# The weight parts' loads on SyncE's queue, ScalarE's copy of the turned keys, a later norm turn and a later pooled-input copy in one decoder layer

## The reference

```python
hn = rmsnorm(h, g_attn_norm[i])
z = hn @ w_in[i]                  # 512 q, 128 k, 128 v, 512 pooled input u
q = rmsnorm(q.reshape(B, S, N_Q_HEADS, HEAD_DIM), g_q[i])
...                               # k likewise; window 128, sinks, shared bias
# multiscale_pool_mixer: trailing mean over 2/4/8/16 positions minus the token,
# then a 128x128 map for each of the 4 groups, and a scale for each channel
y = jnp.einsum('bsgc,gcd->bsgd', pooled, w_pool.astype(jnp.float32))
...
```

## Time and profile before

| | |
|---|---|
| runs | 2050.17, 2062.04, 2053.68 us; median 2053.68 |
| profiled execution | 2053.4 us, span 2051.5 us |
| granted clock of PE | 0.998 of full speed |
| busy | PE 2011.2 us (98%), DVE 67%, ACT 44%, POOL 20% |
| end of the row stages on PE | about 558 us |
| w_lo on DVE (L1554) | 68 of them, 1.287 us in the mean |
| w_parts<-w_split | 88 DMAs of 512 KB on POOL's queue, 4.8 us from issue to landing |

### The profile page before, as it was taken

How to read it: one execution, slowest core, us unless ns; L and a number is a source line. 1 busy time by engine, 2 the same in 40 slices (tenths; PEclk the granted TensorE clock), 3 DMA queues, 4 the chain that set the end, 5 groups by cost and what they waited for, 6 DMA issues and landing times.

```text
span 2051.5 us, 26122 instructions
## 1 busy us (share of the span) xinstructions
PE 2011.2 (98%) x9546; PEld 1663.4 (81%) x9546; DVE 1372.9 (67%) x1920; ACT 899.7 (44%) x1460; POOL 406.5 (20%) x508
## 2 busy tenths in 40 slices
PE   8999999999999999999999999999999999999998
PEld 6887878877788888888888878788888888888877
DVE  4696674767696665655888765966566566987663
ACT  4575754657433333333333543533333333334542
POOL 4454644645410000000000220000000000001310
PEclk9999999999999999999999999999999999999999
DMA  7757566364934223225825128432322328352143
GB/s 193 201 180 245 188 236 219 130 236 131 347 127 130 81 72 103 72 72 171 307 62 165 36 72 223 143 119 67 96 85 72 100 79 292 130 159 78 42 134 103
DMA packets 197387, 292.09 MB, mean 142 GB/s; under 512 B 16139, under 2 KB 118452, under 8 KB 195980
## 3 DMA queue, kind: packets, MB, share of 16 engines
q1 hardware_dynamic: 172672, 212.97, 34.1%
q0 software_dynamic: 22176, 76.96, 10.8%
q10 hardware_dynamic: 2412, 0.50, 0.1%
HBM read 223.25 MB, written 67.51 MB: 142 GB/s over the span
## 4 chain that ended last, share of the span: by engine, by line
PE 84%; DVE 6%; DMA 3%; issue 3%; ACT 2%; POOL 1%; SPq 0%; ACTq 0%; DVEq 0%; POOLq 0%
PE bank L2623 13%; PE bank L2627 13%; PE bank L2625 13%; PE bank L2660 7%; PE bank L2661 7%; PE bank L2662 7%; PE bank L2323 4%; PE bank L2325 4%; PE bank L2324 4%; PE bank L2299 2%; PE bank L2301 2%; PE bank L2300 2%; DMA w_parts<-w_split 1%; PE bank L2392 1%; DVE w_lo L1554 1%
## 5 line engine op out<-in xcount | busy, mean ns | idle before, releaser
L2623 PE MATMUL bank<-a_hi,ring_hi 128*128 128x512 f32 x1232 | 479.7, 389 | 1.0 <-DVE ring_lo L1917 0.7
L2627 PE MATMUL bank<-a_hi,ring_lo 128*128 128x512 f32 x1232 | 479.3, 389 | 0.0
L2625 PE MATMUL bank<-a_lo,ring_hi 128*128 128x512 f32 x1232 | 479.3, 389 | 0.0
L2623 PEld LDWEIGHTS bank<-a_hi,ring_hi 128*128 128x128 f32 x1232 | 231.3, 188 | 49.9 <-DVE ring_lo L1917 1.4
L2625 PEld LDWEIGHTS bank<-a_lo,ring_hi 128*128 128x128 f32 x1232 | 231.3, 188 | 48.0
L2627 PEld LDWEIGHTS bank<-a_hi,ring_lo 128*128 128x128 f32 x1232 | 231.3, 188 | 47.8
L2660 PE MATMUL bank<-d_hi 128*128 128x512 f32 x616 | 239.8, 389 | 0.0
L2662 PE MATMUL bank<-d_hi,d_lo 128*128 128x512 f32 x616 | 239.7, 389 | 0.0
L2661 PE MATMUL bank<-d_lo,d_hi 128*128 128x512 f32 x616 | 239.6, 389 | 0.0
L1376 ACT ACTIVATE d_hi<-keep 128x1024 fp32r<-128x1024 f32 x132 | 139.8, 1061 | 201.9 <-PE bank L2662 184.9
L975 POOL DMA_DIRECT2D hidden_T<-hid x88 | 47.6, 541 | 770.4 <-DVE hid L1953 750.7
(11 more groups left out here) (258 smaller groups left out, 3879.9 us busy)
## 6 DMA issues: line engine op xcount, KB each, us to landing
w_parts<-w_split POOLq DMA_DIRECT2D x88, 512.0 KB, 4.8
hidden_T<-hid POOLq DMA_DIRECT2D x88, 256.0 KB, 2.3
raws<-in_w_gate SPq DMA_DIRECT2D x80, 256.0 KB, 4.7
raws<-in_w_up SPq DMA_DIRECT2D x80, 256.0 KB, 5.1
keep<-hidden_T SPq DMA_DIRECT2D x66, 256.0 KB, 3.8
raw<-in_w_ple_gate SPq DMA_DIRECT2D x64, 256.0 KB, 4.2
keep<-in_w_down SPq DMA_DIRECT2D x44, 256.0 KB, 4.4
other<-hidden_T SPq DMA_DIRECT2D x44, 256.0 KB, 6.8
```

Source lines behind the costliest of these rows:

```text
L2623: mm(dst[:, :], wh[:, g, cols], a_hi[o][:, k, :], start=fresh and k == 0, stop=False, skip_group_check=True)
L2625: mm(dst[:, :], wh[:, g, cols], a_lo[o][:, k, :], start=False, stop=False, skip_group_check=True)
L2627: ins = mm(dst[:, :], wl[:, g, cols], a_hi[o][:, k, :], start=False, stop=k == 3, skip_group_check=True)
```

## The change

Five edits, in the order of the diff:

1. `A_ORDER`, the order in which ACT makes the parts of the feed-forward input, is another.
2. `load_parts` is issued by SP in place of POOL, with the same waits, ahead of what else SP issues for the panel (behind `load_z` and `load_out`). Around it other loads stand elsewhere: the chunks of tile 3 in z(2) and no longer in out(1), the four `load_h(1)` in two panels, the four `load_a(0)` in four panels in place of two.
3. ACT copies the turned keys into SBUF as well (`k_raw`), ahead of `kT_hi`; DVE's `kT_lo` reads this copy; and PE's `transpose_probs`, which writes into the same bank 5, waits for `kT_hi` in place of `kT_lo`.
4. In the tiles 1 to 3 `copy_u` stands behind the half's hosted step, where that step does not begin a new pair of heads. Half 19 is as before.
5. In the gate section the turns of the norm of tile g+1, and what follows from them, stand one panel later.

No edit is to the pooled map itself (`pool_y`, `pool_y_hi`, `pool_y_rest`).

```diff
-A_ORDER = (0, 1, 3, 4, 2, 5, 6)
+A_ORDER = (0, 3, 4, 1, 2, 5, 6)
...
+        k_raw = sb_small("k_raw", [P, P])
...
+            def load_parts(i):
+                kept = (10 + i - OUT_AT[1] if OUT_AT[1] <= i < Z_AT[3] else i - Z_AT[2] if i < Z_AT[3] else
+                        i - Z_AT[3] if i < OUT_AT[2] else 10 + (i - OUT_AT[2]) % 8)
+                if i == SPLIT_END:
+                    sp.wait_ge(lo_done, SPLIT_END)
...
+                else:
+                    sp.wait_ge(panel_used, i - SLOTS_W + 1)
+                sp.wait_ge(parts_stored[kept % 2], 32 * (kept // 2 + 1))
+                for part in range(2):
+                    sp.dma_start(w_parts[parts_slot(i)][:, part, :].bitcast(F32), w_split[kept, part]
+                                   ).then_inc(parts_landed[parts_slot(i)], 16)
...
                 for c in range(10):
                     load_z(t + 1, c)
+                    if t == 1 and c == 0:
+                        load_parts(Z_AT[2] + 1)
+                    if t:
+                        load_parts(Z_AT[t + 1] + c + 2)
...
+                    if t == 1 and c == 9:
+                        for k in range(4):
+                            load_chunk(3, k)
...
                 for c in range(8):
                     load_out(t, c)
-                    if t == 1 and c == 0:
-                        for k in range(4):
-                            load_chunk(3, k)
-                        for b in range(NB):
-                            load_h(1, b)
+                    if t == 0 and c == 7:
+                        load_parts(Z_AT[2])
+                    if t:
+                        load_parts(OUT_AT[t] + c + 2)
+                    if t == 1 and c < 2:
+                        load_h(1, 2 * c)
+                        load_h(1, 2 * c + 1)
...
             for c in range(8):
                 load_out(3, c)
+                if OUT_AT[3] + c + 2 < ROW_PANELS:
+                    load_parts(OUT_AT[3] + c + 2)
                 if c == 0:
                     store_h1(2)
-                if c == 1:
-                    load_a(0, 0)
-                    load_a(0, 1)
-                    load_a(0, 3)
-                if c == 2:
-                    load_a(0, 2)
+                if 1 <= c < 5:
+                    load_a(0, (0, 2, 1, 3)[c - 1])
                 if c == 4:
                     store_n2(2, 0)
                     store_n2(2, 1)
...
-            def load_parts(i):
...
-                    pool.wait_ge(panel_used, i - SLOTS_W + 1)
-                pool.wait_ge(parts_stored[kept % 2], 32 * (kept // 2 + 1))
-                for part in range(2):
-                    pool.dma_start(w_parts[parts_slot(i)][:, part, :], w_split[kept, part]
-                                   ).then_inc(parts_landed[parts_slot(i)], 16)
...
+                if n:
+                    act.wait_ge(kstaged, n)
+                nc.scalar.activation(k_raw[:, :], bank[5][:, 0:P], ACT.Copy)
                 nc.scalar.activation(kT_hi[:, (b + 1) * P:(b + 2) * P], bank[5][:, 0:P],
                                      ACT.Copy).then_inc(k_hi_done, 1)
...
-                nc.vector.tensor_tensor(kT_lo[:, cols], bank[5][:, 0:P], kT_hi[:, cols].bitcast(F32),
+                nc.vector.tensor_tensor(kT_lo[:, cols], k_raw[:, :], kT_hi[:, cols].bitcast(F32),
                                         ALU.subtract).then_inc(kstaged, 1)
...
-                pe.wait_ge(kstaged, 4 * s + min((k + 1) // PAIRS + 1, NB))
+                pe.wait_ge(k_hi_done, 4 * s + min((k + 1) // PAIRS + 1, NB))
...
-                    for g in U_COPY_AT[t > 0].get(half, ()):
+                    fresh = any(has_unit(k, 0) and k % 2 == 0 for _, k in hosted_steps("z", t, half))
+                    u_first = fresh or half == 19 or not late
+                    for g in U_COPY_AT[t > 0].get(half, ()) if u_first else ():
                         copy_u(t, g)
...
                     hosted("z", t, half, Z_AT[t] + half // 2 + 1 if half % 2 == 0 and late else None)
+                    for g in () if u_first else U_COPY_AT[t > 0].get(half, ()):
+                        copy_u(t, g)
...
-                            if r == 1:
+                            if r == 2:
                                 sum_squares(NORM3[g + 1], bank[BS0[0]])
-                            if r == 2:
+                            if r == 3:
                                 normalise3(g + 1, 0)
                                 normalise3(g + 1, 1)
                                 norm3_lo(g + 1, 0)
-                            if r == 3:
                                 norm3_lo(g + 1, 1)
...
-                                if r == 0:
+                                if r == 1:
                                     pe.wait_ge(pp_copied, 8 * g + 4 + 1)
                                     turn_squares(NORM3[g + 1], acc3, bank[BS0[0]])
-                                if r == 1:
+                                if r == 2:
                                     pe.wait_ge(pp_copied, 8 * g + 4 + 2)
                                     turn_rstd(NORM3[g + 1], bank[BS0[1]])
```

More of the change, by code:

```diff
@@ L538, in store_n2 @@
                 sp.dma_start(hnT_d[t, :, 2 * b:2 * b + 2, :], normed(t, b)).then_inc(n2_stored[b % 2], 16)
+            def load_parts(i):
[3 more added lines that the diff above has]
+                    sp.wait_ge(lo_done, SPLIT_END)
+                elif i < SPLIT_END + SLOTS_W:
+                    sp.wait_ge(panel_used, SPLIT_END)
+                    for parity in range(2):
+                        sp.wait_ge(parts_stored[parity], 16 * (SPLIT_END - KEPT_FROM))
+                else:
[4 more added lines that the diff above has]
+                                   ).then_inc(parts_landed[parts_slot(i)], 16)
             def load_bias():
@@ L922, in z_section @@
                 for half in range(20):
-                    if t == 2 and half == 0:
-                        load_parts(Z_AT[2] + 1)
-                    if t >= 2 and half % 2 == 0:
-                        load_parts(Z_AT[t] + half // 2 + 2)
                     if t == 0 and half < 8:
@@ L952, in out_section @@
                 for half in range(16):
-                    if t == 0 and half == 14:
-                        load_parts(Z_AT[2])
-                    if t and half % 2 == 0 and OUT_AT[t] + half // 2 + 2 < ROW_PANELS:
-                        load_parts(OUT_AT[t] + half // 2 + 2)
                     if t < 2:
```

## The result

The changed kernel took 2067.69 us in the median of 7 runs (2066.65 to 2071.84), the kernel before 2052.86 in as many. The ratio is 1.0070, 95% interval 1.0057 to 1.0083: 14.4 us slower (the medians differ by 14.8). I had forecast 2049.5 with a range to 2059, so the sign and the range were wrong. The profiled execution took 2069.46 us, 16.1 more than that of before.

A forecast was written before the change was run, and what follows sets the result against it. PE bounds the kernel, busy 2011.2 of 2051.5 us, leaving 40.3 idle. Terms 3.6 + 4.2 - 2 - 0.5 - 1.4 = 3.9 us less than 2053.4 gave 2049.5 us, range 2043 to 2059.

The forecast's parts named there:

- What SP issues later: Norm stores behind parts on SP: 2 us more at the feed-forward start, 0.5 more in z(2) and z(3).
- The feed-forward start: First weights wait for stores behind panel 68's parts, leaving about 9 us ahead instead of 13.8: 2 us more, 0 to 9.
- A_ORDER: Feed-forward input: reordered ACT copies that no listed wait depends on; nothing gained or lost.
- The parts: Row stages: parts issued by SP end PE's waits for w_parts, 3.9 us, plus 0.3 behind them: 4.2 us less, 0 to 5.2.
- The rival with one queue and no gain: Parts queue behind SP's earlier transfers, so their stalls stay or move; parts' term nought, 2053.7 us, chance 0.14.
- Keys' copy and u copy: Attention in z(1) and z(3): stalls near 131, 153, 370 and 470 shrink; 3.6 us less, between 1.8 and 6.
- my 1.2 at 370 and 0.6 at 470: Keys' copy: logits start once qT_lo is ready, no longer after the kT_lo wait; 1.2 and 0.6 us less.
- The two waits for u at the pooled map: Behind the moved u copy, bank freed 2 to 4 us later, pooled sums later: nothing, up to 1 us lost.
- The norm turn: Two gate stages: PE still waits for w_lo, with transposes left to do; 1.4 us more, from 1 less to 4 more.
- The slower rival: Feed-forward start late because raws wait for norm stores that wait for panel 68: 2056.5 us, chance 0.16.
- its point of decision: Feed-forward start: the late start decides once first raws go less than about 6 us ahead of PE's start.

The follow-up runs named there:

- The first: The changed kernel with tile 3's chunk 4 to 7 loads in out(1) one panel earlier, ahead of the panel's weight parts: 2056.13 us, ratio 1.0013.
- third run: The kernel before with only the weight parts issued by SP and the loads placed as in the change: 2069.28 us, ratio 1.0072.
- ninth run: The changed kernel with chunk loads and out(3) norm stores ahead of parts, and the last two a_raw loads one panel earlier: 2053.41 us, ratio 0.9997.
- twelfth run: The kernel before with parts on SP, chunk loads, norm stores and a_raw loads earlier, and the new a_hi order; no other edit: 2053.84 us, ratio 0.9997.
- eighth run: The kernel before with only the gate section's norm turn one panel later: 2055.85 us, ratio 1.0016.
- fourth run: The kernel before with only the u copy moved behind the hosted step: 2051.80 us, ratio 0.9991.

## Why the prediction was wrong

**What SP issues later: the step that failed.** The term that I put at nothing is that of the chunk loads. I wrote that "SP now waits for PE at each panel from z(2) on, and what stands behind a pair of parts waits too", and then counted norm stores only. The chunk loads of out(1) stand behind such pairs, four of them, and there the load has no lead at all. I gave it nothing; it cost 9.6 us in the stretch from 320 to 346, and 12.9 when the 3.3 us of its first wait, ahead of 320, are counted in. The first and the third run settle it.

**The feed-forward start.** The mechanism was right, stores behind a pair of parts and the weights behind the stores, and I put it at 2 us with an upper bound of 9. It was 6.4. The pair for panel 70 left at 550.25, 16.3 us ahead of the start without PE's own wait, as I had worked out (16.4). But the pair and the two stores behind it took SP until 553.29 to issue, for which I had nothing, and the weights left 8.3 us behind them where I had 7.4. Part of the difference is another item of the same kind: I had costed the spread a_raw loads as a help for the parts and not as a delay for ACT. In the runs the stores are worth 3.0 us (6.9 to 3.9), 1.7 of it clock, and the a_raw loads 1.4 (3.9 to 2.5). In the ninth run's trace PE's waits from 536 to 600 are 1.45 us for the last parts and 0.82 for cg, so nearly all of the last 2.5; no run takes them away.

**A_ORDER.** "Moves copies on ACT that no row above waits for: nothing." It is worth 2.0 us in one pair of traces, by longer waits (4.2 us in place of 2.9) and a lower clock behind them, though the times of the two runs do not tell them apart. The reason is that the order of the loads changed with it: one edit could only be priced together with the other.

**The parts.** The waits in the earlier trace rows went, as forecast, 4.0 us. But 1.0 to 2.0 us came back at the next meeting of DVE and POOL, and in the mended version a wait for the last pair. By these figures the net was 0.3 (4.0 less 2.0 less 1.7) to 3.0 us (4.0 less 1.0) and not 4.2. The rival with one queue and no gain named the right net for the twelfth run, not by its mechanism: the list of the changed kernel has no wait for parts at all. What I quoted of the Trainium skill, "DMA: Bandwidth & Descriptors", section "Queues, rings and completion order", does not show as a cause here: from issue to landing the parts took 4.6 us on SP's queue and 4.8 on POOL's, in the median.

**Keys' copy and u copy.** At 131 and 153 the sum was right, 1.8 us in the table as forecast, but not its parts: the u copy alone gives 2.6 there, and the keys' copy alone nothing (its next wait took the gain back, and by 162.93 PE stood where it had stood at 162.83). That the two together give 0.8 less than the u copy alone was not taken apart. Behind that, my 1.2 at 370 and 0.6 at 470 supposed that the panel's matmuls stand between the turn and the logits as before, so that PE would meet qT_lo just when it was ready. PE, relieved of one wait, comes earlier to the next: at 381.69 it waited 1.47 us for qT_lo, at 480.39 1.68. What is won is the difference of the old wait and the new: 0.46 us at 370 (1.93 less 1.47) and nothing at 470 (1.46 before, 1.68 after). The two waits for u at the pooled map, 3.3 us, I had bounded at 1 us, since I asked when the bank is free for the next panel and not who else writes to it.

**The norm turn.** 1.4 us forecast. The sign and the wait were right. The size is less sure: the last column of the table is 1.4 in the changed kernel and 3.0 in the eighth run, its mean is 1.6 in the seven kernels with the later turn and -1.0 in the six without it (with such pieces of clock on both sides), and the interval of the eighth run begins at 1.4. So the forecast is at the lower edge of what was measured.

**The slower rival** named the place of the second loss, and 7 us more than my sum, where 6.4 were measured in all; its point of decision was passed too, for the weights left 7.0 us ahead of the start, 5.0 without PE's own wait, and it asked for less than 6. I gave it 0.16. The first and larger loss was in none of my rivals, though the order of SP's queue shows it.

## What to carry to other kernels

When loads that wait for PE are put into a queue that others share, go down the queue and write beside each item behind them the panel at which it now leaves and the panel in which it is needed; an item with less than its landing time between the two is a stall in a loop, and loads without such waits belong ahead. Price a wait that is taken away only up to the next wait of the same engine: what the producer behind it is late by stays. And orders that follow each other (loads, and the copies that consume them) are one edit.

## What the runs showed of the hardware

A loop of waits costs more than its idle time. PE waited 3.15, 0.50 and 4.27 us between 317 and 340, 7.9 us together, and the granted clock was 0.83 over the 30 us from 320, that is, for part of them 1.2 and not 2.4 GHz, which is another 5.1 us. The sum is the 12.9 us that were lost, within 0.1. Behind one short wait the clock did not always fall: 0.83 over 10 us behind 1.93 us of waiting in the kernel before, 1.00 behind 1.94 at the same place in the fourth run.

A DVE subtraction that starts within an add of POOL ended a fixed time behind that add. One of 128x256 (mix_lo) takes 0.42 us alone. In all nine kernels with parts on SP, at the place shown for the twelfth, it took 1.50 to 1.52 and ended 0.28 to 0.29 us behind the add. One of 128x1024 (w_lo) takes 1.23 us alone. Where it started within POOL's add it ended 1.08 to 1.09 us behind it, 65 times in the fourteen traces, whether it had started 0.3 or 1.25 us ahead of the add's end; the 2.22 us of the earlier trace rows are one of these. So its duration tells how much of the add was left.
